# Expert outputs of a mixture-of-experts layer: weighted and accumulated in DRAM by the scatter, instead of combined on VectorE at the end

## The reference, cut to what matters

```python
combine = einsum('tk,tke->te', weights, one_hot(expert_id, 16))      # 2 experts per token
for e in experts:                                                     # 1024 -> 256 -> 1024
    out = out + (silu(t @ w_gate[e]) * (t @ w_up[e]) * combine[:, e, None]) @ w_down[e]
x = x + out
return rms_norm(x, norm_final_w)
```

## Time and profile before

| | |
|---|---|
| median of three runs | 695.23 us |
| the profiled execution | 695.14 us |
| its span (first to last instruction or transfer) | 693.4 us |
| mean granted TensorE clock | 0.972 of full speed |
| expert part, from the first gather of tokens to the last product | 429.7 to 663.9 us |
| from there to the end | 663.9 to 693.4 us |

### The profile page before, as it was taken

One profiled execution on the slowest core, in us unless ns is written; L12 is line 12 of the kernel. 1 busy time (PEld: TensorE's weight loads), 2 busy tenths in 40 slices (PEclk: granted clock), 3 DMA queues, 4 the chain that ended last, 5 costly groups with the idle time before them and its releaser, 6 DMA issues.

```text
span 693.4 us, 9261 instructions
## 1 busy us (share of the span) xinstructions
PE 640.7 (92%) x3376; PEld 535.8 (77%) x3376; DVE 472.7 (68%) x781; ACT 396.5 (57%) x673; POOL 175.6 (25%) x216
## 2 busy tenths in 40 slices
PE   4999999999999999999999997999999999998920
PEld 4788788788878888988888886788878888887810
DVE  5778995364621444424764557999899999997827
ACT  7439584255623332335342355479898899987713
POOL 7000008982000000000000001144545655455210
PEclk9999999999999999999999999799999999999975
DMA  8523334113222211111325815568787797866345
GB/s 270 184 97 62 61 100 129 62 60 77 66 61 62 61 61 60 62 61 61 121 72 211 324 41 207 170 206 283 227 257 254 231 308 236 304 220 217 105 152 230
DMA packets 73744, 104.63 MB, mean 151 GB/s; under 512 B 31649, under 2 KB 53218, under 8 KB 73570
## 3 DMA queue, kind: packets, MB, share of 16 engines
q1 hardware_dynamic: 60928, 95.57, 42.2%
q0 software_dynamic: 12672, 8.43, 4.0%
q10 hardware_dynamic: 98, 0.03, 0.0%
HBM read 123.90 MB, written 17.83 MB: 204 GB/s over the span
## 4 chain that ended last, share of the span: by engine, by line
PE 81%; DVE 10%; DMA 3%; ACT 3%; issue 2%; SPq 0%; POOLq 0%; ACTq 0%; DVEq 0%
PE bank L1628 22%; PE bank L1630 21%; PE bank L1629 21%; PE bank L2049 2%; PE bank L1778 2%; DVE down_lo L1388 1%; PE bank L1686 1%; DMA expert_rows<-expert_rows_hbm 1%; PE bank L1967 1%; DMA x_T<-in_x 1%; PE bank L1847 1%; PE bank L1837 1%; DVE rank_onehot L1504 1%; PE bank L1797 1%; DMA ew_raw<-in_w_gate,extra_weight_rows 1%
## 5 line engine op out<-in xcount | busy, mean ns | idle before, releaser
L1628 PE MATMUL bank<-h_hi,w_hi 128*128 128x512 f32 x304 | 123.9, 408 | 1.3 <-DVE h_lo L1091 1.3
L1630 PE MATMUL bank<-h_hi,w_lo 128*128 128x512 f32 x304 | 119.4, 393 | 0.0
L1629 PE MATMUL bank<-h_lo,w_hi 128*128 128x512 f32 x304 | 119.0, 391 | 0.0
L1388 DVE TENSOR_TENSOR gate_up_lo<-ew_raw,gate_up_hi 128x1024 fp32r<-128x1024 f32 x92 | 108.5, 1220 | 8.4 <-ACT gate_up_hi L967 8.1
L703 POOL DMA_INDIRECT unit_tokens<-ffn_rows,row_index x23 | 32.5, 1413 | 296.8 <-DVE row_index L1512 285.4
L967 ACT ACTIVATE gate_up_hi<-ew_raw 128x1024 fp32r<-128x1024 f32 x92 | 92.2, 1056 | 7.8 <-DMA ew_raw<-in_w_gate,extra_weight_rows 7.1
L1069 DVE TENSOR_TENSOR w_lo<-w_raw,w_hi 128x2048 fp32r<-128x2048 f32 x26 | 60.4, 2323 | 49.9 <-ACT w_hi L758 49.7
L1628 PE MATMUL bank<-gate_up_hi,unit_in_hi 128*128 128x512 f32 x184 | 76.6, 416 | 0.6 <-DVE unit_in_lo L1539 0.6
L1630 PE MATMUL bank<-gate_up_hi,unit_in_lo 128*128 128x512 f32 x184 | 72.7, 395 | 0.0
L1629 PE MATMUL bank<-gate_up_lo,unit_in_hi 128*128 128x512 f32 x184 | 72.6, 395 | 0.0
L1628 PEld LDWEIGHTS bank<-h_hi,w_hi 128*128 128x128 f32 x304 | 57.6, 190 | 13.2 <-issue 2.1
(11 more groups left out here) (364 smaller groups left out, 1295.3 us busy)
## 6 DMA issues: line engine op xcount, KB each, us to landing
w_raw<-in_w_in SPq DMA_DIRECT2D x16, 1024.0 KB, 5.2
ew_raw<-in_w_gate SPq DMA_DIRECT2D x32, 512.0 KB
ew_raw<-in_w_up SPq DMA_DIRECT2D x32, 512.0 KB
ew_raw<-in_w_down SPq DMA_DIRECT2D x32, 512.0 KB
w_raw<-in_w_out SPq DMA_DIRECT2D x4, 1024.0 KB, 5.0
expert_rows<-expert_rows_hbm SPq DMA_DIRECT2D x8, 512.0 KB, 7.2
x_T<-in_x SPq DMA_DIRECT2D x4, 512.0 KB, 5.3
w_raw<-in_w_in SPq DMA_DIRECT2D x8, 256.0 KB, 4.3
```

Source lines behind the costliest of these rows:

```text
L1388: dve.tensor_tensor(dst, eraw[slot][:, :], hi.bitcast(F32), ALU.subtract).then_inc(elo_done, 1)
L1628: pe.matmul(out_ap, lhs_hi, rhs_hi, start=first, stop=False)
L1629: pe.matmul(out_ap, lhs_hi, rhs_lo, start=False, stop=False)
L1630: return pe.matmul(out_ap, lhs_lo, rhs_hi, start=False, stop=last)
```

## The change

The rows of a unit are multiplied by their slot's weight as they leave PSUM and then added in DRAM to a copy of the residual by a scatter that accumulates. What is read back at the end is the finished sum.

- SyncE writes the residual's four tiles to `token_sums_hbm`, each ahead of the store of the same tile to `ffn_rows`.
- The weights of all tokens (128 x 8) are transposed on TensorE in pass 0 after unit_in(1), copied by ScalarE in its pass 0, and written to a DRAM column of 1024 numbers by a DMA from ScalarE's queue.
- `weigh(u)`, a new indirect gather, brings the 128 weights of unit u into column u of `uw` (zero for empty slots); there are 23.
- `unit_out` and `unit_out_half` scale by that column and wait for its gather.
- `spread(u)` goes to the token's row, accumulates, and waits on GpSimd until `spread(u-1)` has landed (the first one: until the residual is written).
- GpSimd's loop is reordered: gate weights, token rows, down weights, scatter, up weights, then the gather of the column.
- At the end SyncE reads four tiles instead of eight transfers; `add_experts` is gone, and so is SyncE's wait for `gu_ps`.

```diff
-        o_rows = nc.dram_tensor("expert_rows_hbm", (2 * S, D), F32)
+        sum_rows = nc.dram_tensor("token_sums_hbm", (S, D), F32)
+        wt_rows = nc.dram_tensor("slot_weights_hbm", (2 * S, 1), F32)
...
             for t in range(TT):
+                sp.wait_ge(y_done, TT + t + 1)
+                sp.dma_start(sum_rows[t * P:(t + 1) * P, :], y[:, t, :]).then_inc(residual_out, 16)
                 if t < TT - 1:
                     sp.wait_ge(t_scaled, t + 1)
...
-            sp.wait_ge(gu_ps, UNITS)
             for t in range(TT):
-                for k in range(2):
-                    sp.dma_start(pair[k][:, t, :], o_rows[S * k + t * P:S * k + (t + 1) * P, :]).then_inc(pair_in[t], 16)
+                sp.dma_start(y[:, t, :], sum_rows[t * P:(t + 1) * P, :]).then_inc(sums_in[t], 16)
...
+                if u:
+                    pool.wait_ge(ot_out[(u - 1) % 2], 16 * ((u - 1) // 2 + 1))
+                else:
+                    pool.wait_ge(residual_out, 16 * TT)
                 nc.gpsimd.indirect_dma_start(
-                    out=o_rows[:, :], out_offset=bass.IndirectOffsetOnAxis(ap=ridx[:, SEQ[u], 0:1], axis=0),
+                    out=sum_rows[:, :], out_offset=bass.IndirectOffsetOnAxis(ap=ridx[:, SEQ[u], 1:2], axis=0),
                     in_=ot[u % 2][:, :], in_offset=None,
-                    bounds_check=2 * S - 1, oob_is_err=False).then_inc(ot_out[u % 2], 16)
+                    bounds_check=S - 1, oob_is_err=False, compute_op=ALU.add).then_inc(ot_out[u % 2], 16)
+
+            def weigh(u):
+
+                pool.wait_ge(ids_done, 1 + batch_of(SEQ[u]))
+                nc.gpsimd.indirect_dma_start(
+                    out=uw[:, u:u + 1], out_offset=None, in_=wt_rows[:, :],
+                    in_offset=bass.IndirectOffsetOnAxis(ap=ridx[:, SEQ[u], 0:1], axis=0),
+                    bounds_check=2 * S - 1, oob_is_err=False).then_inc(wt_in[u % 4], 16)
 
             pool.wait_ge(rows_out, 16 * TT)
             for u in range(4):
                 fetch(u)
+            pool.wait_ge(wt_out, 16)
+            for u in range(3):
+                weigh(u)
             for u in range(UNITS):
+                load_extra(KIND_G, u + 4)
                 if u + 4 < UNITS:
                     fetch(u + 4)
+                load_extra(KIND_D, u + 2)
                 spread(u)
-                load_extra(KIND_G, u + 4)
-                load_extra(KIND_D, u + 2)
                 load_extra(KIND_U, u + 4)
+                if u + 3 < UNITS:
+                    weigh(u + 3)
...
             def unit_out(u):
                 act.wait_ge(dn_ps, u + 1)
+                act.wait_ge(wt_in[u % 4], 16 * (u // 4 + 1))
...
-                    ins = act.activation(ot[u % 2][:, S * h:S * (h + 1)], ps[down_banks(u)[h]][:, :], ACT.Copy)
+                    ins = act.activation(ot[u % 2][:, S * h:S * (h + 1)], ps[down_banks(u)[h]][:, :], ACT.Copy, scale=uw[:, u:u + 1])
...
+                if u == 0:
+                    act.wait_ge(wt_turned, 1)
+                    act.activation(w12_f[:, :], ps[1][0:2 * TT, 0:P], ACT.Copy).then_inc(wt_turned, 1)
+                    act.wait_ge(wt_turned, 2)
+                    act.dma_start(wt_rows[:, :].rearrange("(r p) o -> r (p o)", p=P), w12_f[:, :]).then_inc(wt_out, 16)
...
-                act.wait_ge(tok_added, t + 1)
+                act.wait_ge(sums_in[t], 16)
...
-            def add_experts(t):
-
-                dve.wait_ge(pair_in[t], 32)
-                link(dve.scalar_tensor_tensor(y[:, t, :], pair[0][:, t, :], w1[:, t:t + 1], y[:, t, :], ALU.mult, ALU.add))
-                dve.scalar_tensor_tensor(y[:, t, :], pair[1][:, t, :], w2[:, t:t + 1], y[:, t, :],
-                                         ALU.mult, ALU.add).then_inc(tok_added, 1)
...
-                dve.tensor_copy(ot[u % 2][:, S:], ps[down_banks(u)[1]][:, :]).then_inc(half_done, 1)
+                dve.tensor_scalar(ot[u % 2][:, S:], ps[down_banks(u)[1]][:, :], uw[:, u:u + 1], None, ALU.mult).then_inc(half_done, 1)
...
-            add_experts(0)
-            for t in range(1, TT):
-                add_experts(t)
-                final_norm(t - 1)
-            final_norm(TT - 1)
+            for t in range(TT):
+                final_norm(t)
...
+                if u == 0:
+                    pe.wait_ge(choice_step, WEIGHTS_SET)
+                    pe.transpose(ps[1][0:2 * TT, 0:P], w12[:, :, :].rearrange("p k t -> p (k t)"), ident[:, :]).then_inc(wt_turned, 1)
+                if u == 1:
+                    pe.wait_ge(wt_turned, 2)
```

More of the change, by code:

```diff
@@ L197, in build @@
         nffn = at("norm_ffn_b", [P, D], F32, r_tmp + 8192)
-        pair = [at(f"expert_rows{k}", [P, TT, D], F32, r_main + 16384 * k) for k in range(2)]
         out_t = at("out_T", [P, TT, D], F32, ffn_raw)
@@ L217, in build @@
         e1, e2, e12 = rt("first_onehot", [P, TT, EG]), rt("second_onehot", [P, TT, EG]), rt("both_onehot", [P, TT, EG])
-        m1, m2, dif, w1, w2 = (rt(n_, [P, TT]) for n_ in ("first_logit", "second_logit", "logit_gap", "first_weight", "second_weight"))
+        m1, m2, dif = (rt(n_, [P, TT]) for n_ in ("first_logit", "second_logit", "logit_gap"))
+        w12 = rt("slot_weights", [P, 2, TT])
         sel = rt("chosen", [P, TT, NG, EG])
@@ L286, in build @@
         brg = new("router_bias", [P, NG + NE])
+        w12_f = new("slot_weights_F", [2 * TT, P])
+        uw = new("unit_weights", [P, UNITS])
         row_rep = at("index_row_repeated", [P, P, 16], BF16, tri_at)
@@ L349, in build @@
         hid_hi, hid_lo, dn_ps, ot_done = sem("hidden_hi_done"), sem("hidden_lo_done"), sem("down_ps"), sem("unit_out_done")
-        pair_in = [sem(f"expert_rows_in{t}") for t in range(TT)]
-        tok_added = sem("y_added")
+        sums_in = [sem(f"token_sums_in{t}") for t in range(TT)]
+        residual_out, wt_turned, wt_out = sem("residual_rows_out"), sem("slot_weights_turned"), sem("slot_weights_out")
+        wt_in = [sem(f"unit_weights_in{i}") for i in range(4)]
         pool_set = sem("gpsimd_set")
@@ L356, in build @@
         choice_step = sem("choice_step")
-        GD_IN, ED_IN, SEL_DONE, EXPERTS_KNOWN = range(1, 5)
+        GD_IN, ED_IN, SEL_DONE, WEIGHTS_SET, EXPERTS_KNOWN = range(1, 6)
         choice_exp = sem("choice_exp")
@@ L645, in _ @@
             nc.gpsimd.memset(ones[:, :], 1.0)
+            link(nc.gpsimd.memset(uw[:, :], 0.0))
             link(nc.gpsimd.memset(tri[:, :], 1.0))
@@ L1528, in _ @@
             dve.wait_ge(choice_exp, ED_OUT)
[L1529 to L1532, removed]
+            link(dve.tensor_scalar(w12[:, 0, :], dif[:, :], 1.0, None, ALU.add))
+            link(dve.reciprocal(w12[:, 0, :], w12[:, 0, :]))
+            link(dve.tensor_tensor(w12[:, 0, :], w12[:, 0, :], gp[:, :], ALU.mult))
+            dve.tensor_tensor(w12[:, 1, :], w12[:, 0, :], dif[:, :], ALU.mult).then_inc(choice_step, 1)
             row_ids(4)
@@ L1594, in _ @@
                         one_hots(EARLY + u)
-            def add_experts(t):
-                dve.wait_ge(pair_in[t], 32)
-                link(dve.scalar_tensor_tensor(y[:, t, :], pair[0][:, t, :], w1[:, t:t + 1], y[:, t, :], ALU.mult, ALU.add))
-                dve.scalar_tensor_tensor(y[:, t, :], pair[1][:, t, :], w2[:, t:t + 1], y[:, t, :],
-                                         ALU.mult, ALU.add).then_inc(tok_added, 1)
             def unit_out_half(u):
                 dve.wait_ge(dn_ps, u + 1)
+                dve.wait_ge(wt_in[u % 4], 16 * (u // 4 + 1))
                 dve.wait_ge(ot_out[u % 2], 16 * (u // 2))
-                dve.tensor_copy(ot[u % 2][:, S:], ps[down_banks(u)[1]][:, :]).then_inc(half_done, 1)
+                dve.tensor_scalar(ot[u % 2][:, S:], ps[down_banks(u)[1]][:, :], uw[:, u:u + 1], None, ALU.mult).then_inc(half_done, 1)
             unit_out_half(UNITS - 1)
```

## The result

The changed kernel takes 701.22 us (median of 7 runs; the kernel before in the same runs 695.53), a ratio of 1.0086 (95% interval 1.0057 to 1.0114). The forecast was 684.3 us. Its profiled execution took 700.81 us with a span of 699.1, 5.7 more than before.

A forecast was written before the change was run, and what follows sets the result against it. TensorE was taken to bound the loop, and a serial 29.5 us the end; 695.14 - 7.9 (end) - 3.0 (TensorE's pauses) = 684.2, plus 0.1 for the median: 684.3 us, range for all 681 to 690.

The forecast's parts named there:

- The end: After TensorE's last product: four reads replace eight and VectorE's sums go; -10.5 + 0.4 + 2.2 = -7.9 us.
- S + 11.2: S is SyncE's issue of the first read at the end; scaling would end 11.2 us later, against 21.7 before.
- The accumulation: Last scatter's read of its target at the end: taken as 1.5 us, a second pass of the same bytes; at most 5.2.
- The new wait at the end: Last scatter must wait until place 21's has landed, so it starts 0.7 us later, or not later at all.
- TensorE's pauses: In the loop, the new order brings down and gate weights earlier, ending pauses of 2.20 and 0.83 us: -3.0 us together.
- what is put into the loop: Loop additions: 23 column gathers, the scatter's second read, ScalarE's scaled copy; all expected to fit in idle time or DMA room.
- the landing outgrows a unit: Rival, chance 0.08: landings L past 8.3 us hold GpSimd's queue, adding 22 x (L - 8.3); 711 us at L = 10.
- Its sum, 5.2 + 1.5 + 1.5 = 8.2: Rival's loop landing in us: 5.2 for an empty DMA among loads, 1.5 data, 1.5 reading; bound 9.34 - 1.02 = 8.3.
- A single late one is taken up by GpSimd's idle half: Argument against the slower rival: one late scatter landing in the loop costs nothing, as GpSimd idles half its time.
- The Trainium skill's figure: HBM access 0.2 us average, 2 at high load: loaded scatter 2 us longer than the quiet one, so the slower rival stays away.
- The columns and the stores: 23 column gathers (1.3 us each) fit GpSimd's idle time; SyncE's four more stores fill its wait for the norm.
- The start: Before the loop: the weights' transpose, copy, DMA issue, extra stores and first column gathers fall into waits; cost nothing.

The follow-up runs named there:

- f1: The changed kernel with each scatter accumulating only the left 512 numbers of its rows, half the bytes, into a separate DRAM tensor: 687.2 us, 0.987 of before.
- e1: The kernel before with only GpSimd's order changed (gate weights, token rows, down weights, scatter, up weights), scatters plain: 692.3 us, 0.9963 of before.
- e4: The changed kernel without the 23 column gathers and their waits, every row weighted by 1: 701.6 us, 1.0078 of before.
- f3: The changed kernel with extra units' gate, down and up weights and two token gathers issued ahead of the scatter: 705.6 us, 1.0164 of before.

## Why the prediction was wrong

- **The end: right but for one size.** S + 11.2 became 684.57 to 696.02, 11.5; from S to the end of the span 14.5 where 14.6 was forecast. *The accumulation* was taken as 1.5 us, "the row with the same bytes at the same quiet place"; it is 3.2. It goes mostly by bytes (f1), but not as one more pass at the pace of the first: two passes would be at most 3.0 us for the 0.32 MB, and it took 3.75. The two source reads of a reduction, as the Trainium skill has them (Collectives: The Full Stack, "The bandwidth ceiling: the fold count and why AG ≠ RS ≠ AR"), have the sign, but a factor of two is less than this trace shows.
- **The new wait at the end: right.** The scatter of place 21, empty, landed 2.7 us after its start, and the last one came 2.0 us after TensorE's end instead of 1.6: 0.4 us, where 0.7 was forecast.
- **TensorE's pauses: right by themselves** (e1, -2.8 us in the loop against -3.0). In the changed kernel both are gone too, but others stand in their place.
- **What failed is "what is put into the loop".** The scatter's second read was priced at nothing, as room on the DMA engines, and not as time to land in a queue that waits for it; the loop came out 9.9 us longer than before where 3.0 less was forecast, and 12.7 longer than e1's. The room was there: the DMA engines' share in the loop is 0.73 against 0.71. The rival with the right mechanism stood there, "the landing outgrows a unit", with 0.08. Three things put it too low. Its sum, 5.2 + 1.5 + 1.5 = 8.2, was within 0.1 of its own bound of 8.3 and still got small odds on the ground that most landings would be shorter. The bound left out the 0.84 us from release to start that the same text uses at the end, and the issue itself, 1.02 us plain, takes 1.65 (up to 2.6) when accumulating. And full scatters among the loads take 6.3 to 9.9 us from start to landing, where 9.34 - 0.85 = 8.5 is the most that a unit holds; seven take longer, and neighbours start up to 10.7 us apart. Its formula put a delay on each of the 22 scatters that have a neighbour before them; nine did start on a landing, and the loop lost 9.9 us. (The formula itself gives 684.3 + 22 x 1.7 = 721.7 us at L = 10, not the 711 written there.)
- **"A single late one is taken up by GpSimd's idle half": wrong.** The up weights' slack behind the scatter was what counted: ScalarE waits for them five times, 5.0 us at most. That GpSimd is idle at other times, when it waits for VectorE (25.2 us in the loop ahead of the extra units' weights), didn't help them.
- **The Trainium skill's figure** (DMA: Bandwidth & Descriptors, "Latency and other measured facts": 2 us of access to HBM at high load) had counted against this rival. The trace has 6.3 to 9.9 us for a full scatter among the loads and 6.4 for the last one, alone: from nothing to 3.5 us more, so the estimate of 2 us lies inside what was measured, and the longest landings lie above it.
- **The columns and the stores: right**; e4 without columns is no faster. The start was forecast to cost nothing; the 2.4 us before the third silu lie within what kernels with the same start differ by (464.9 to 468.0), so this term is neither borne out nor refuted.

## What to carry to other kernels

Price a DMA twice: by what it takes of the engines, and by the time until it has landed, from start to start if a queue waits for it; when the second comes near the period of the loop, some of the landings will pass it (nine of 22 here), and a worst case that fits by 0.1 us is no small risk. A wait in a queue that serves several consumers can be paid by any of them, so give a waiting DMA what lets it not wait (another target, a neighbour that can't collide) before reordering what is behind it: in f3, putting the urgent things first made the waits longer.

## What the hardware showed that I had not expected

- An accumulating scatter of some 0.32 MB to DRAM moved at about 85 GB/s when alone, where the plain one has up to 295 (mean of a slice): 6.4 us from start to the next engine's reaction against 3.25, 4.75 with half the bytes. Each issue took GpSimd 1.55 to 2.6 us (median 1.65), where the plain one took 0.98 to 1.95 (median 1.02).
- An indirect DMA whose rows are all left out still took its place in the queue: the up weights of empty units landed 8.4 us after their second issue behind an accumulating scatter.
- TensorE's granted clock was 0.66, a mean between its two levels of 1.2 and 2.4 GHz, from 630 to 635, after 5 us in which the engine was busy for 3.08. From 653 to 658 it was 1.00, though the engine had been busy for only 2.37 of the 5 us before.
